# Weight sums of a seven-product down projection: made once and kept in DRAM, with the square of relu on ScalarE

## What is computed

```python
def ffn_sublayer(x, g_pre, w_up_l, w_down_l, g_post):
    h = rmsnorm(x, g_pre)
    a = jax.nn.relu(jnp.einsum('btd,df->btf', h, w_up_l))
    return x + rmsnorm(jnp.einsum('btf,fd->btd', a * a, w_down_l), g_post)
```

## Time and profile before

| | |
|---|---|
| median of 3 runs | 2736.45 us (2733.47 to 2742.29) |
| the profiled execution, its own time | 2740.59 us |
| its span | 2738.8 us |
| PE busy | 2546.8 us (93%) |
| DVE busy | 1710.4 us (62%) |
| ACT busy | 1075.3 us (39%) |
| POOL busy | 1036.0 us (38%) |
| mean granted TensorE clock | 0.973 |
| moved by DMA | 373.73 MB |

### The profile page before, as it was taken

One profiled execution on the slowest core, in us unless ns is written; L12 is line 12 of the kernel. 1 busy time (PEld: TensorE's weight loads), 2 busy tenths in 40 slices (PEclk: granted clock), 3 DMA queues, 4 the chain that ended last, 5 costly groups with the idle time before them and its releaser, 6 DMA issues.

```text
span 2738.8 us, 35159 instructions
## 1 busy us (share of the span) xinstructions
PE 2546.8 (93%) x13562; PEld 2181.6 (80%) x13562; DVE 1710.4 (62%) x2687; ACT 1075.3 (39%) x1810; POOL 1036.0 (38%) x602
## 2 busy tenths in 40 slices
PE   7999999999999898899988999878999978999995
PEld 6899999899995577787777777766777867799884
DVE  6331112365662346988878786487888378777778
ACT  4001110386775444344444333333434244433432
POOL 1200000275753663243334454333446242533323
PEclk9999999999999999999999999989999999999997
DMA  5312323499969853434434443435443342433341
GB/s 177 108 40 73 111 67 112 97 178 157 189 99 295 242 179 136 138 108 169 144 117 156 169 133 125 152 102 171 159 139 121 126 155 91 159 119 112 108 161 63
DMA packets 264109, 373.73 MB, mean 136 GB/s; under 512 B 78676, under 2 KB 199068, under 8 KB 259032
## 3 DMA queue, kind: packets, MB, share of 16 engines
q1 hardware_dynamic: 243410, 263.37, 34.4%
q10 hardware_dynamic: 14518, 89.43, 9.4%
q0 software_dynamic: 6016, 18.68, 2.4%
HBM read 323.39 MB, written 103.76 MB: 156 GB/s over the span
## 4 chain that ended last, share of the span: by engine, by line
PE 69%; DVE 13%; issue 6%; POOL 4%; ACT 3%; DMA 3%; SPq 2%; ACTq 0%; DVEq 0%; POOLq 0%
PE ml_y L2104 16%; PE ml_up L2028 7%; PE ml_up L2030 7%; PE ml_up L2029 7%; PE pj_acc L481 6%; PE pj_acc L483 5%; PE pj_acc L482 5%; PE at_o L1150 4%; PE ml_y L2061 3%; POOL ml_w_lo L1917 3%; DVE ml_w_lo L2454 2%; DVE ml_a_lo_raw L2403 2%; PE at_turn L1130 2%; DVE em_raw L2448 2%; PE at_score L1119 1%
## 5 line engine op out<-in xcount | busy, mean ns | idle before, releaser
L1917 POOL TENSOR_TENSOR ml_w_lo<-em_raw,ml_w_hi 128x1024 fp32r<-128x1024 f32 x160 | 430.1, 2695 | 759.5 <-ACT ml_w_hi L2139 759.5
L2139 ACT CAST ml_w_hi<-em_raw 128x1024 fp32r<-128x1024 f32 x384 | 402.3, 1048 | 383.4 <-PE ml_y L2104 245.3
L2028 PE MATMUL ml_up<-ml_h_hi,ml_w_hi 128*128 128x512 f32 (+2 forms) x1280 | 456.7, 357 | 21.3 <-DVE ml_w_lo L2454 21.2
L2029 PE MATMUL ml_up<-ml_h_lo,ml_w_hi 128*128 128x512 f32 (+2 forms) x1280 | 454.0, 355 | 0.0
L2030 PE MATMUL ml_up<-ml_h_hi,ml_w_lo 128*128 128x512 f32 (+2 forms) x1280 | 453.7, 354 | 0.0
L2104 PE MATMUL ml_y<-ml_w_hi,ml_a_hi 128*128 128x512 f32 x896 | 369.1, 412 | 83.6 <-DVE em_hx L2482 30.4
L2104 PE MATMUL ml_y<-ml_w_lo,ml_a_hi 128*128 128x512 f32 x896 | 360.7, 403 | 0.0
L2104 PE MATMUL ml_y<-ml_w_hi,ml_a_lo 128*128 128x512 f32 x896 | 359.9, 402 | 0.0
L2454 DVE TENSOR_TENSOR ml_w_lo<-em_raw,ml_w_hi 128x1024 fp32r<-128x1024 f32 x224 | 289.0, 1290 | 78.7 <-ACT ml_w_hi L2139 77.1
L481 PE MATMUL pj_acc<-pj_h_hi,pj_w_hi 128*128 128x424 f32 (+1 forms) x800 | 290.4, 363 | 6.1 <-DVE pj_h_lo L699 6.1
L2028 PEld LDWEIGHTS ml_up<-ml_h_hi,ml_w_hi 128*128 128x128 f32 x1280 | 243.4, 190 | 61.5 <-DVE ml_w_lo L2454 30.3
(11 more groups left out here) (315 smaller groups left out, 4546.4 us busy)
## 6 DMA issues: line engine op xcount, KB each, us to landing
em_raw<-in_w_up SPq DMA_DIRECT2D x64, 1024.0 KB, 5.4
em_raw<-in_w_down SPq DMA_DIRECT2D x64, 1024.0 KB, 5.3
out_o_a_k_s<-in_cache_a_k ACTq DMA_DIRECT2D x8, 3060.0 KB, 11.7
out_o_a_v_s<-in_cache_a_v ACTq DMA_DIRECT2D x8, 3060.0 KB, 11.5
em_raw<-scratch_pt SPq DMA_DIRECT2D x34, 512.0 KB, 7.4
em_raw<-in_w_out SPq DMA_DIRECT2D x16, 1024.0 KB, 5.1
scratch_pt<-pj_proj SPq DMA_DIRECT2D x10, 1056.0 KB, 4.1
pj_w<-in_w_in SPq DMA_DIRECT2D x20, 512.0 KB, 4.0
```

Source lines behind the costliest of these rows:

```text
L1917: nc.gpsimd.tensor_tensor(split_of(w_lo, n), raw_of(n), f32(split_of(w_hi, n)), ALU.subtract).then_inc(w_lo_ready, 1)
L2028: pe.matmul(out, hi[:, k, :], h_hi[:, k, cols], start=(k == 0), stop=False)
L2029: pe.matmul(out, hi[:, k, :], h_lo[:, k, cols], start=False, stop=False)
L2139: nc.scalar.copy(split_of(w_hi, n), raw_of(n)).then_inc(w_hi_ready, 1)
```

## The change

1. **Sums once.** During the input projection POOL loads `w_down` in 16 steps of 1 MB (half a part each), makes the four sums with three operations and stores the 1 MB into a new DRAM tensor `wt`. Two steps are put behind the gain multiplication of each block from 9 to 16. SP waits for the last store before it loads the first keys.
2. **Loads by product.** In the feed-forward part each product's 128x1024 block is loaded by a DMA of its own (0.5 MB), from `w_down` for P1, P2, P3 and from `wt` for P7, P6, P5, P4. Two products share a slot of `raw`; P3 is alone in one. `w_sum` and its semaphore are gone.
3. **Square on ACT.** ACT squares the relu in place; DVE's `hidden` is gone. PE takes an up bank again once relu has read it.
4. **P4 before P3**, and the last part's closing order is (2, 3, 4, 0, 1) in place of (4, 0, 1, 2, 3).

The split between DVE and POOL stays as it was: seven and four per part.

```diff
+            def load_sums(n):
+                if n >= SUM_STEPS:
+                    return
+                if n >= 2:
+                    pool.wait_ge(sums_out, 16 * (n - 1))
+                frm = down_v[n // 2][:, n % 2::2, :]
+                pool.dma_start(sums[:, n % 2].rearrange("p (f h) c -> p f (h c)", h=2), frm).then_inc(sums_in[n % 2], 16)
+
+            def sum_weights(n):
+                at = sums[:, n % 2]
+                load_sums(n + 1)
+                pool.wait_ge(sums_in[n % 2], 16 * (n // 2 + 1))
+                nc.gpsimd.tensor_tensor(at[:, 1, :], at[:, 3, :], at[:, 1, :], ALU.subtract).then_inc(summed, 1)
+                pool.wait_ge(summed, 3 * n + 1)
+                nc.gpsimd.tensor_tensor(at[:, 0, :], at[:, 1, :], at[:, 0, :], ALU.add).then_inc(summed, 1)
+                pool.wait_ge(summed, 3 * n + 2)
+                nc.gpsimd.tensor_tensor(at[:, 2:4, :], at[:, 2:4, :], at[:, 0:1, :].to_broadcast([P, 2, D // 2]),
+                                        ALU.subtract).then_inc(summed, 1)
+                pool.wait_ge(summed, 3 * n + 3)
+                pool.dma_start(d["wt"][n // 2, n % 2], at).then_inc(sums_out, 16)
...
             for i in range(5, FBLK):
                 scale_weights(i)
+                if i == SUMS_FROM:
+                    pool.wait_ge(conv_out, 64)
+                    load_sums(0)
+                if SUMS_FROM <= i and n < SUM_STEPS:
+                    sum_weights(n)
+                    sum_weights(n + 1)
+                    n += 2
...
-    P1, P7, P2, P6, P5, P3, P4 = range(7)
+    P1, P7, P2, P6, P5, P4, P3 = range(7)
...
-    LO_BY_POOL = (P1, P7, P2, P6)
-    BY_DVE, BY_POOL = (P1, P7, P2, P6, P5), (P3, P4)
-    CLOSING_ORDER = (MT - 1, *range(MT - 1))
+    LO_BY_DVE = (P5, P4, P3)
+    BY_DVE, BY_POOL = (P1, P7, P2, P6, P5), (P4, P3)
+    CLOSING_ORDER = (2, 3, 4, 0, 1)
...
+                for step in LOADS[load]:
+                    product = step[3]
+                    if product in SUM:
+                        frm = d["wt"][part][:, :, SUM[product], :].rearrange("q p c -> p q c")
+                    else:
+                        frm = down_v[part][:, TOP[product]:TOP[product] + DF, LEFT[product]:LEFT[product] + HALF]
+                    sp.dma_start(raw_of(UNIT_OF[step]), frm).then_inc(landed, 16)
...
                     last.then_inc(relu_done, 1)
+                    act.wait_ge(relu_done, up_banks(step) - len(chunks(g)) + c + 1)
+                    last = nc.scalar.activation(to, to, ACT.Square)
...
+                    last.then_inc(hidden_done, 1)
...
-                    last = nc.vector.scalar_tensor_tensor(at, src[:, 0:at.shape[1] * HT].rearrange("p (q t) -> p q t", t=HT), 0.0, at,
-                                                          ALU.max, ALU.mult)
...
                         if i == DF:
                             first_sums(step)
-                            w_sum(step, P7)
...
-                        if i == PF - 1:
-                            w_sum(step, P6)
-                            w_sum(step, P5)
-                        hidden(step)
```

More of the change, by code:

```diff
@@ L1561, in out_and_mlp @@
             latest[bank] = q
-    LOADS = []
+    LOADS, LOAD_OF, LANDED = [], {}, []
     for step in UNITS:
         kind, g, part, i = step
[L1566 to L1577, removed]
+        if kind != "down" and i % 2 == 0:
+            LOADS.append((step, (kind, g, part, i + 1)))
+        if kind == "down" and i in (P1, P2, P5):
+            LOADS.append((step, (kind, g, part, i + 1)))
+        if kind == "down" and i == P3:
+            LOADS.append((step,))
+    for n, load in enumerate(LOADS):
+        LOAD_OF.update({step: n for step in load})
+        parts = len(load) if load[0][0] == "down" else 1
+        LANDED.append(16 * parts + (LANDED[n - RAW] if n >= RAW else 0))
     SLOTS = (("up", 0, 2), ("down", 0, P1), ("down", 0, P2), ("up", 1, 1), ("down", 0, P3), ("up", 1, 2), ("up", 1, 3))
@@ L1729, in turn_his, with up_banks, wait_emptied, wait_turned @@
             return sum(banks_of(s) for s in STEPS[:STEPS.index(step)] if s[0] in ("turn", "h"))
+        def up_banks(step):
+            return sum(banks_of(s) for s in UNITS[:UNIT_OF[step] + 1] if s[0] == "up")
+        UP_OF = [step[0] == "up" for step in STEPS for _ in range(banks_of(step))]
+        def wait_emptied(engine, count):
+            ups = sum(UP_OF[:count])
+            if count > ups:
+                engine.wait_ge(emptied, count - ups)
+            if ups:
+                engine.wait_ge(relu_done, ups)
+        def wait_turned(engine, step):
+            wait_emptied(engine, turns_through(step))
+        def wait_hidden(engine, step):
+            engine.wait_ge(hidden_done, up_banks(step))
         def conv_parts(g):
@@ L1747, in lo_by_dve @@
         def lo_by_dve(n):
-            return UNITS[n][0] == "up" or UNITS[n][0] == "down" and UNITS[n][3] not in LO_BY_POOL
+            return UNITS[n][0] == "up" or UNITS[n][0] == "down" and UNITS[n][3] in LO_BY_DVE
         DVE_LOS = [sum(lo_by_dve(m) for m in range(n + 1)) for n in range(NU)]
@@ L2132, in split_hi @@
                 kind, g, part, i = step
-                if kind == "down" and i in (P7, P6, P5, P4):
-                    act.wait_ge(w_summed, 4 * part_of(step) + (P7, P6, P5, P4).index(i) + 1)
-                else:
-                    wait_loaded(act, load_of(step))
+                wait_loaded(act, LOAD_OF[step])
                 if n >= SPLIT:
@@ L2627, in _ @@
                         split_lo(n + AHEAD)
-                        if n + AHEAD < NU and UNITS[n + AHEAD][0] == "down" and UNITS[n + AHEAD][3] == P3:
-                            w_sum(UNITS[n + AHEAD], P4)
                     if kind == "up":
```

155 lines of the change are left out of this document (64 added, 91 removed).

## The result

The changed kernel takes **2664.2 us** (median of 4 runs, 2662.6 to 2667.5) against 2735.9 for the kernel before (4 runs, one more than in the table above): ratio 0.9736, 95% interval 0.9717 to 0.9755. It is 71.7 us faster where 88 were forecast, inside the range. The profiled execution took 2663.37 us, its span is 2661.6.

What follows compares the result with a forecast made beforehand. Matmuls bound the last group; in the first three, PE loses time waiting on DVE and POOL, which wait for each other. Steady parts 24 plus heads 64 make 88 us off 2736.45: 2648 us, range 2598 to 2704.

Steps and rivals of the forecast that it cites:

- The square's cover: Feed-forward parts: the cast behind each square comes 0.6 us later, covered by at least 5.4 us, so no cost.
- Steady parts: 15 parts of the first three groups without norms beside the products: 24 us gained, bounds 16 and 32.
- The part of 40.8 to 41.2 us: Sign to look for: the time of each steady part in the first group after the change.
- Heads: 10 parts in which norms run beside the products: 64 us gained, 6.4 per part, bounds 16 and 123.
- DVE gets 12.3 us per part: Time DVE is spared per part: 9.4 us from weight sums and their waits, 2.9 from the square.
- 280 to 310: Sign to look for: DVE's total busy time falls by this many us.
- P4 before P3: Steady parts: PE's wait between P5 and the next product goes, 15 waits of 1.1 us, 16.5 us.
- Sums on POOL: Input projection: POOL falls 9 us behind over 8 blocks, hidden by its 31.4 us lead, cost 0.
- loads: Feed-forward parts: 5.5 MB per part in place of 4, some 29 of 41 us, cost taken as 0.
- The rival of starved DMAs: Projection: DVE's operations hold up POOL's DMA issues, PE stands for 66 us, 2714 us; chance 0.02.
- The end: Closing order of the last part: order and products change places, taken as 0 with 5 us either side.
- The rival "norms set the pace": The untouched norm chain over POOL, ACT and DVE limits the norm-laden parts to 20 us gained: 2692 us; chance 0.22.

Runs made afterwards that it cites:

- square_dve: The changed kernel with relu's square on DVE again, read from PSUM: 2648.4 us, ratio 0.9688 to the kernel before.
- no_sums: The changed kernel without the weight-sum stage in the projection, every product's block loaded straight from `w_down`: 2665.1 us, ratio 0.9751 to the kernel before.
- adds_first: The changed kernel with DVE adding a product's banks ahead of the low split of the unit two further on: 2737.6 us, ratio 1.0004 to before.

## Why the prediction was right, and where its sum was not

- **The square's cover (priced 0; the failed step).** "Its unit is two units off, at least 5.4 us, so the cover is there" looked at PE only. The cast is also what DVE's in-order queue stands on, and the additions that PE wants within a microsecond are behind it. Its place on ACT costs 13 to 16 us (square_dve), while the prediction counted its 2.9 us per part as gain.
- **Steady parts (24).** Measured 21.4, and 3.9 lost in the last group, which I had put at 48.7 us per part still. The 24 was too small for what it described, order and sums: without the square on ACT the 15 parts gain 32.6 us (752.5 to 719.9). Then came 11.2 for the square. The part of 40.8 to 41.2 us was missed at 41.4; square_dve has it, 41.0.
- **Heads (64).** Measured 50.7. "About half of what DVE gets should reach PE" was too much: the sums alone give 30 to 32 us of the 94 us that they take from DVE in ten parts, a third. On the other side I priced the order at nothing in the heads, where it gives 21 us. The mechanism of the earlier trace rows, a sum waiting for POOL's split, is real but small: 13 us as a wait by itself.
- **"DVE gets 12.3 us per part" as the measure.** Its busy time fell by 227.8 us, not 280 to 310, since other operations stretched: P1's low part went from 0.68 us (the median before) to 2.13 on average, for it now begins beside a split of POOL's (at 1189.66 it takes 2.90 us beside a split that POOL began at 1189.17). As the earlier trace rows showed before, an operation that meets another on the other engine waits for it. The Trainium skill, page "SBUF — State Buffer", section "SBUF: two separate sides", calls this an exclusive lock on a shared port pair; the row of 2.70 us agrees (DVE's split waits until POOL's first one ends), while the 4.9 us per part that the rule could have given on top did not come: POOL's 160 splits take 2.62 us on average, 2.70 before.
- **P4 before P3 (right in kind).** The wait between P5 and the next product is gone, and nothing is late there in its place. Worth 39 to 42 us, not 16.5, and 68 with the square on ACT. In the steady parts the size was near, 19.6 to 20.3 us; what was left out is as much again in the heads.
- **Sums on POOL (0), loads (0): right.** no_sums differs by 0.9 us. I had POOL fall up to 9 us behind, hidden by its lead; it fell 9.8 us behind at most and was hidden. The rival of starved DMAs did not occur: the 32 issues took 0.59 to 0.77 us. The case of 3.1 us in the Trainium skill, same page and section, is one in which DVE holds the shared ports; DVE was busy for 48 of 240 us here, so it is not tested. No cast of weights in the feed-forward part waited for a load at all, where 20 had waited 42.2 us for `w_up` before; I had not counted that as a gain. The 0.5 MB from `wt` land in 4.8 us.
- **The end (0 within 5): right**, 2.9 us.
- **The rival "norms set the pace"** is not needed: moving the residuals changed nothing. What it rested on is still there: PE waits 24.6 us for POOL's splits, 26.9 before, and 17 to 26 us in the other versions.

So the direction and the main mechanism, DVE out of PE's way, were right, and the size was partly luck. By pieces, the 88 us were 16.5 for the order, some 15 for the square (2.9 of 12.3 of the heads' 64) and 57 for the sums. The runs give 40 to 42, -16 and 46 to 47 (by the medians). The forecast came within 16 us because an order undersized by 24 us stood against a square of the wrong sign, 31 us apart, and sums 11 us too dear.

## What to carry to other kernels

Where engines issue strictly in order, price a moved operation by what stands *behind* it in each queue and how soon that is wanted, not by the slack of its own result: 0.6 us put ahead of a cast cost 0.4 to 1.0 us per steady part with P4 first and 1.0 to 2.1 with P3 first, through a split and an addition on another engine that was idle at the time. An accumulation onto a bank that another engine must empty first belongs as far as possible behind the product that filled it; with a queue-bound consumer that reordering alone was worth nearly as much as taking 300 us of work and waiting off the engine. And when a change has several pieces, time the combinations: here one piece ate a fifth of what the others brought.

## What I had not expected of the hardware

Shifting DVE's low splits by one operation moved them onto POOL's: in adds_first the 224 splits take 1.48 us on average in place of 1.32, 28 of them more than 2.3 and up to 3.15, and DVE shows 56 us more busy time for the same work. Busy time of DVE or POOL is therefore no fixed price of an instruction; it includes the rest of the other engine's operation when the two meet.
